# Half of the last prompt tile is gathered with the sample; the second expert table becomes the stationary operand

## The reference, cut to what matters

```
h = h + concat(mixers(rmsnorm(h) @ w_in)) @ w_out
# PEER: 8 heads, 128 x 128 = 16384 experts, 16 chosen per head
q   = (rmsnorm(h) @ wq).reshape(tokens, 8, 2, 64)
s   = einsum('thpd,hpnd->thpn', q, keys)          # 2 x 128 scores per head
top 16 of each side, top 16 of the 16 x 16 sums   # e = i1 * 128 + i2, gate = softmax
act = gelu(sum_d x[t, d] * u_tab[e, d])
h   = h + sum over 8 heads x 16 of gate * act * v_tab[e]
# PLE
h   = h + sigmoid(rmsnorm(h) @ w_gate) * (p @ w_ple)
```

## Time and profile before

| | |
|---|---|
| median of 3 runs | 4154.75 us |
| the profiled execution | 4150.1 us, of it 4148.3 us between the first and the last instruction (the span) |
| TensorE (PE) busy | 98% of the span |
| VectorE (DVE) | 68% |
| GpSimd (POOL) | 44% |
| ScalarE (ACT) | 37% |
| DMA | 858.82 MB, mean 207 GB/s |

### The profile page before, as it was taken

The page is one execution under the profiler, slowest core; times in us unless marked ns, Lnnn a source line. Parts: engine busy times, 40 slices in busy tenths (PEclk is TensorE's granted clock), DMA queues, the critical chain, the costliest instruction groups (busy, mean ns, idle before and its releaser), DMA issues.

```text
span 4148.3 us, 56638 instructions
## 1 busy us (share of the span) xinstructions
PE 4065.6 (98%) x22010; PEld 3474.2 (84%) x22010; DVE 2828.2 (68%) x4773; ACT 1525.8 (37%) x2323; POOL 1844.4 (44%) x1196
## 2 busy tenths in 40 slices
PE   8999999999999999999999999999999999999999
PEld 6788599999999987888477876999999999878883
DVE  5765369936888677777367552799268886677763
ACT  1442155543333333333314312555433333333333
POOL 0131068887777563111001310788877774721110
PEclk9988999999999999999999889999999999999999
DMA  3201156667888999997022011566678889899970
GB/s 122 47 12 47 53 174 216 212 214 243 306 299 306 328 314 335 325 328 266 27 63 38 12 72 41 179 227 212 210 244 308 313 294 339 297 340 326 325 243 23
DMA packets 389291, 858.82 MB, mean 207 GB/s; under 512 B 88352, under 2 KB 236064, under 8 KB 385312
## 3 DMA queue, kind: packets, MB, share of 16 engines
q1 hardware_dynamic: 266144, 578.11, 41.6%
q0 software_dynamic: 67584, 201.57, 14.0%
q10 hardware_dynamic: 55296, 75.52, 5.0%
HBM read 723.51 MB, written 131.54 MB: 206 GB/s over the span
## 4 chain that ended last, share of the span: by engine, by line
PE 75%; DVE 14%; POOL 6%; issue 2%; ACT 2%; DMA 1%; SPq 0%; ACTq 0%; DVEq 0%; POOLq 0%
PE banks L1337 21%; PE banks L1404 20%; PE banks L820 7%; PE banks L1384 4%; PE banks L1260 3%; PE banks L1434 3%; POOL u_stage L2046 3%; PE banks L1278 2%; PE banks L1349 2%; DVE peer_scores L2571 2%; POOL u_stage L2039 1%; DVE peer_scores L2593 1%; PE banks L1113 1%; DVE peer_scores L2568 1%; PE banks L1101 1%
## 5 line engine op out<-in xcount | busy, mean ns | idle before, releaser
L1404 PE MATMUL banks<-v_parts,gated_parts 128*128 128x512 f32 x4608 | 1048.0, 390 | 7.8 <-DVE gated_parts L2730 6.2
L1404 PEld LDWEIGHTS banks<-v_parts,gated_parts 128*128 128x128 f32 x4608 | 865.6, 188 | 189.3 <-issue 9.7
L2031 POOL DMA_INDIRECT peer_gates<-peer_v,u_stage x384 | 533.3, 1389 | 833.2 <-DVE normed L2726 574.8
L1337 PE MATMUL banks<-peer_x_parts,u_parts 128*128 128x448 f32 x3168 | 663.7, 367 | 0.0
L1337 PEld LDWEIGHTS banks<-peer_x_parts,u_parts 128*128 128x128 f32 x3168 | 589.5, 188 | 44.5
L1897 ACT ACTIVATE v_parts<-v_stage 128x1024 fp32r<-128x1024 f32 x256 | 271.4, 1060 | 582.1 <-PE banks L1404 580.3
L2709 DVE TENSOR_TENSOR v_parts<-v_stage,v_parts 128x1024 fp32r<-128x1024 f32 x256 | 313.4, 1224 | 247.2 <-ACT v_parts L1897 247.1
L1337 PE MATMUL banks<-peer_x_parts,low_s 128*128 128x448 f32 x1696 | 398.5, 367 | 0.0
L2039 POOL DMA_INDIRECT u_stage<-gelus,u_stage x256 | 350.5, 1369 | 77.7 <-issue 77.7
L1823 ACT ACTIVATE u_stage<-banks 128x448 f32<-128x448 f32 x256 | 138.9, 542 | 656.5 <-PE banks L1337 641.1
L2686 DVE SCALAR_TENSOR_TENSOR normed<-peer_gates,u_stage,normed 128x1024 f32<-128x1024 f32 x254 | 326.4, 1285 | 60.6 <-DMA peer_gates<-peer_v,u_stage 47.6
(11 more groups left out here) (347 smaller groups left out, 6797.5 us busy)
## 6 DMA issues: line engine op xcount, KB each, us to landing
v_stage<-peer_v SPq DMA_DIRECT2D x256, 512.0 KB, 5.1
u_stage<-peer_ut SPq DMA_DIRECT2D x244, 512.0 KB, 5.4
dense_gelus<-u_stage ACTq DMA_DIRECT2D x256, 224.0 KB
gates<-peer_gates SPq DMA_DIRECT2D x16, 3072.0 KB, 12.1
u_stage<-gates SPq DMA_DIRECT2D x64, 768.0 KB, 6.8
gated<-dense_gelus SPq DMA_DIRECT2D x256, 192.0 KB, 5.7
x<-peer_ut SPq DMA_DIRECT2D x64, 512.0 KB, 5.0
u_raw<-peer_ut SPq DMA_DIRECT2D x64, 512.0 KB, 5.3
```

The costliest lines, as they stand in the source:

```text
L1337: ins = mm(PS[:, d % 2, 0:DW], u_part(n, a, k), XR[:, b, k, DENSE0:TOK], start=(k == 0 and m == 0), stop=(k == KT - 1 and m == 2))
L1404: ins = mm(vo[2 * t + half], HR[:, s, a, t * 128:(t + 1) * 128], VR[:, s, b, half * 512:(half + 1) * 512], start=(j == 0 and m == 0), stop ...
L2031: eng.indirect_dma_start(out=GU[:, t % 4, :], out_offset=None, in_=din["peer_v"].rearrange("l i j d -> (l i j) d"), in_offset=bass.Indirec ...
```

## The change

Three things are changed together.

1. The second half of tile 3 (64 tokens) leaves the dense path and joins the sample (`SPLIT`, `ACROSS`). The gathered tile now has 128 tokens on 128 partitions and `SLOTS` = 128 slots; the sample is scored with all 8 heads, and tile 3 with its heads in two halves, as the sample was before. Tile 3's first 64 tokens stay dense, so 320 columns instead of 384 are gated (`PW3`), scattered (40 units, `GBLK` = 40) and multiplied. The dense rows of the first table keep their 448 columns.
2. In the third stage the roles are exchanged: the table row is stationary in 8 chunks of 128 features, the 320 gated columns move. Per row that is 8 x 3 = 24 matmuls of 320 columns into all 8 PSUM banks. The result stands features by tokens. ACT copies the 8 banks to `VOT`, and TensorE turns them back, tile by tile, in the PLE stage (`down_turned`). Tile 0 is turned there too, because no bank is free before.
3. The gathers are placed anew. `GV` is 4, so 124 slots of tile 0 are added in the second stage. The 128 slots of the gathered tile are added from row 12 on, 8 in 7 rows (`PICKED`). POOL gathers 32 weights first (`WEIGHTS_AHEAD`), then a row and a weight in turn; DVE waits for the weights in 8 groups of 16 instead of once for all. The fold matmuls are gone.

The core of the diff:

```diff
-PW3 = 128 * len(SPREAD)
-GBLK = 48
+PW3 = sum(ACROSS.values())
+GBLK = 40
...
-A_PAIRS = [9, 12, 12, 12, 11]
+A_PAIRS = [13, 13, 13, 11, 7]
 LAST_PAIRS = range(sum(A_PAIRS), PAIRS)
-GV = 17
+GV = 4
...
-SLOTS = 64
+SLOTS = 128
...
+PICKED = 12
+WEIGHTS_AHEAD = 32
...
-        return [m for m in range(SLOTS) if WEIGHED + m * 3 // 2 == j]
+        return [m for m in range(SLOTS) if PICKED + m * 7 // 8 == j]
...
+            def picked_scores():
+
+                for g in range(4):
+                    pe.wait_ge(*bank_free())
+                    b = fill("sc", L, SAMPLE, g)
+                    p, r = g % 2, slice(64 * (g % 2), 64 * (g % 2) + 64)
+                    for n in range(4):
+                        h = 4 * (g // 2) + n
+                        if p == 0:
+                            pe.wait_ge(act_done, at("drained", "qt", L, h, "s"))
+                        for to, c0 in ((slice(0, 64), SEQ), (slice(64, 128), COL[SPLIT] + 64)):
+                            ins = mm(b[to, n * 128:(n + 1) * 128], QT[r, h, c0:c0 + 64], KEYS[r, h, :], start=True, stop=True)
+                    pe.did(ins.then_inc(pe_done, 1), "filled", "sc", L, SAMPLE, g)
...
-            vo = [fill("vo", L, i, half) for i in SPREAD for half in range(2)]
+            vc = [fill("vc", L, k) for k in range(KT)]
             for j in range(NKEYS):
                 s = j % NVB
                 pe.wait_ge(v_low, NKEYS * L + j + 1)
                 pe.wait_ge(h_low, NKEYS * L + j + 1)
-                for t, i in enumerate(SPREAD):
-                    for half in range(2):
-                        for m, (a, b) in enumerate(PARTS):
-                            ins = mm(vo[2 * t + half], HR[:, s, a, t * 128:(t + 1) * 128],
-                                     VR[:, s, b, half * 512:(half + 1) * 512],
-                                     start=(j == 0 and m == 0), stop=(j == NKEYS - 1 and m == 2))
-                        if j == NKEYS - 1:
-                            pe.did(ins.then_inc(pe_done, 1), "filled", "vo", L, i, half)
+                for k in range(KT):
+                    for m, (a, b) in enumerate(PARTS):
+                        ins = mm(vc[k][:, 0:PW3], VR[:, s, b, k * 128:(k + 1) * 128], HR[:, s, a, :],
+                                 start=(j == 0 and m == 0), stop=(j == NKEYS - 1 and m == 2))
+                    if j == NKEYS - 1:
+                        pe.did(ins.then_inc(pe_done, 1), "filled", "vc", L, k)
                 if j < NKEYS - 1:
                     ins.then_inc(v_done, 1)
-                if j == TURN_ROW:
-                    turn(3 * L + 2, GATHER)
-            pe.wait_ge(row_used, ALL_SLOTS * (L + 1))
-            for half in range(2):
-                pe.wait_ge(*bank_free())
-                b = fill("vo", L, SAMPLE, half)
-                ins = mm(b[0:SAM, :], const("fold"), XN[:, 1, half * 512:(half + 1) * 512], start=True, stop=True)
-                pe.did(ins.then_inc(pe_done, 1), "filled", "vo", L, SAMPLE, half)
-
+
+            def down_turned(t):
+
+                i = SPREAD[t]
+                w = ACROSS[i]
+                for half in range(2):
+                    pe.wait_ge(act_done, at("drained", "vc", L, 4 * half + 3))
+                    pe.wait_ge(*bank_free())
+                    b = fill("vo", L, i, half)
+                    for k in range(4):
+                        ins = eng.transpose(b[0:w, k * 128:(k + 1) * 128], VOT[:, 4 * half + k, t * 128:t * 128 + w], ident)
+                    pe.did(ins.then_inc(pe_done, 1), "filled", "vo", L, i, half)
+
+            turn(3 * L + 2, GATHER)
...
+            down_turned(0)
...
-            act.wait_ge(pe_done, at("filled", "vo", L, SAMPLE, 1))
+            act.wait_ge(v_low, NKEYS * (L + 1))
+            for k in range(KT):
+                copy_out(("vc", L, k), VOT[:, k, :], lambda b: b[:, 0:PW3])
+            act.wait_ge(dve_done, at("picked", L))
...
-            for m in range(4, GV):
-                for s in range(SLOTS * (m - 4) // (GV - 4), SLOTS * (m - 3) // (GV - 4)):
-                    gather_weight(s)
-                gather_row(GSLOTS - GV + m)
+            for s in range(WEIGHTS_AHEAD):
+                gather_weight(s)
             for s in range(SLOTS):
                 gather_row(GSLOTS + s)
+                gather_weight(s + WEIGHTS_AHEAD)
...
-                if j == WEIGHED:
-                    dve.wait_ge(weights_gathered, 16 * SLOTS * (L + 1))
-                    dve.did(TT(WGT, WGT, GATE, ALU.mult).then_inc(dve_done, 1))
-                    dve.wait_ge(dve_done, count("dve_done"))
...
+                    if m % CHUNK == 0:
+                        c = slice(m, m + CHUNK)
+                        dve.wait_ge(d_picked[m // CHUNK], 16 * CHUNK * (L + 1))
+                        dve.did(TT(WGT[:, c], WGT[:, c], GATE[:, c], ALU.mult).then_inc(dve_done, 1))
+                        dve.wait_ge(dve_done, count("dve_done"))
...
+            dve.wait_ge(row_used, ALL_SLOTS * (L + 1))
+            dve.did(TT(H[0:SAM, SAMPLE, :], H[0:SAM, SAMPLE, :], XN[0:SAM, 1, :], ALU.add).then_inc(dve_done, 1), "h", 3 * L + 2, SAMPLE)
+            dve.did(TT(H[64:128, SPLIT, :], H[64:128, SPLIT, :], XN[64:128, 1, :], ALU.add).then_inc(dve_done, 1), "picked", L)
             turned(3 * L + 2, GATHER)
-            add_h(L, SPREAD[-1], 1, "vo", 3 * L + 2)
-            for half in range(2):
-                add_h(L, SAMPLE, half, "vo", 3 * L + 2)
+            add_down(1)
+            scale(3 * L + 2, 1)
```

91 lines of the change are left out of this document (54 added, 37 removed).

## The result

The changed kernel takes 4171.45 us (median of 8 runs, 4161.41 to 4187.67), the kernel before 4152.53 us beside it (8 runs, 4143.37 to 4155.88). The ratio is 1.0047, interval 1.0029 to 1.0064: slower by half a per cent, where 4080 us was forecast. The profiled execution took 4161.41 us and has a span of 4159.4 us, against 4148.3 before.

A forecast was written before the change was run, and what follows sets the result against it. TensorE was taken to bound the kernel, and DMA the changed third stage from row 12. Per layer 26.5 + 14.2 - 1 - 1 - 1.2 = 37.5 us, 75 for both, off 4154.75: 4080 us, range 4025 to 4150.

The forecast's parts named there:

- term 2: Third stage: DMA paces from row 12 on, 1.45 MB per row at 385 GB/s, 3.77 us; 168.3 MB in 437 us.
- term 1: Third stage, TensorE: a matmul of 320 columns takes 146 ns, so 24 per table row take 3.50 us against 4.08.
- term 3: Third stage, DVE: 3.31 us of work a row, no bound, with 0.2 to 0.45 us to spare.
- Term 4: Third stage, first gathered row: 32 weights stand before it, so TensorE waits some 18 us (bounds 8 and 22).
- Term 5: Second stage: 8 units go, 14.2 us saved; gathers and DMA fit, 1 us put on irregular waits.
- Term 6: First stage: the half tile is searched last and the new table of pairs costs 1 us, bounds -2 and 8.
- Term 7: Begin of the PLE: turning the sums back and scaling two banks cost 1.2 us more than before.
- The clock: Third stage: TensorE will be slow for some us behind the new wait, but DMA paces the rows and covers it.
- B: Third stage: DMA gives only 345 GB/s, the stage takes 552 us, the whole 4182 us; chance 0.13.
- "DVE busy without a gap": Sign against the forecast: DVE has no gap while DMA is not full, meaning term 3 was too small.

The follow-up runs named there:

- e9_pointer: Changed kernel with the table's low part on DVE by scalar_tensor_tensor, its scalar read from a column of ones in SBUF: 4110.92 us.
- e1: Changed kernel with only the first 32 of a layer's 128 weights gathered and used four times over, 96 commands fewer: 4108.16 us.
- e10: Changed kernel with the second half of the table's low part left out from row 4 on (L2744 on 512 columns): 4104.37 us.
- e2_half_table: Changed kernel with every second row of the second table not loaded in the third stage, from the fifth row on: 4171.41 us.

## Why the prediction was wrong

**The step that failed** is in term 2: "from row 12 on DMA paces the stage", 3.77 us a row. The third stage's sum sets DMA against TensorE (term 1) and DVE (term 3) and has no bound of POOL, though from row 12 on 8 rows and 8 weights have to be gathered in 7 rows. With the price that I had, 1.37 us per gather command from the chain, used in terms 4 and 5 as if it belonged to the command, such a bound would have come out at 2 x 1.37 x 8/7 = 3.13 us and hidden. So the price failed as well: in its place the runs showed 1.57 + 0.30 = 1.87 us per command from row 12 to 96, and POOL's commands as the pace, 4.29 us a row. The earlier trace rows are from a stage in which DVE was busy for 71% of the time; from 1550 to 1800 us of the changed kernel it is 79%. In the third stages of the kernel before 2 of 282 commands took over 2.5 us, in those of the changed kernel 78 of 512.

What it cost: from row 12 to 96 a row takes some 4.29 us instead of 3.77, 84 x 0.52 = 44 us. The third stage is 543.1 us against the 501 forecast, 42 us more, and 540.6 in layer 2. e9_pointer gives 26 us of it back. The other 16 us are the size of term 2: to the end of e9_pointer's stage the 168.3 MB took about 455 us from 1510 on, 370 GB/s on average instead of 385. DMA is not full behind the wait (359 GB/s from 1510 to 1550 us) and in the last rows (229 from 1920 on).

Point by point:

- Term 1, matmul: right (146 ns forecast, 42 us for 288).
- Term 2, DMA: the ceiling was right (381 to 389 GB/s in e1, e9 and e10 at shares of 1.04 and 1.05), the mean over the stage 4% too high, and DMA was not the pace.
- Term 3, DVE: nearly right as a bound on itself (busy for 3.41 us a row, 3.31 forecast), it had gaps (L2762 waited 77.4 us for gathers in layer 1's third stage). What I missed is that its instructions lengthen another engine's.
- Term 4, the wait: 18 forecast, 18.3 and 18.1 measured. Part of this is luck: in layer 1 the 32 weights took 1.47 us each instead of 1.37 (1447.27 to 1494.41 us), and the first of them came 1.8 us earlier in the stage than forecast.
- Term 5, second stage: 7.8 and 7.5 us saved instead of 13.2; the 5.5 us are one wait of 6.0 us at its begin in each layer, gone with LEAD 18. I had the mean rate of the gathers and not the time at which the first rows land.
- Term 6: -2.7 and +0.3 us, the first a little outside the bounds of -2 to 8. Term 7: 1.7 us for 1.2. The sum has a slip here: 0.87 us for the turn of tile 0 were taken off, though they are part of the 527 us against which 501 were set. Without it the term would have been 2.1 us.
- The clock: the stage's 0.94 comes from short stretches at the 1.2 GHz level behind idle times of TensorE, the longest of them around the idle time of 18.3 us (0.56 on average from 1485 to 1504 us). The kernel before, busy throughout, is at 1.00 in the earlier trace rows. The chain from 1550 to 1800 us has no piece of TensorE, so the clock was not what paced the rows there. What it added elsewhere was not separated.

The sum of the misses, against the profiled execution: in layer 1 42.1 (third stage) + 5.4 (second) - 3.7 (first) + 0.5 (PLE) = 44.3 us, in layer 2 39.6 + 5.7 - 0.7 + 0.5 = 45.1 us, and the stages ahead of the experts came out 3.7 us shorter than before: 85.7 us. 4150.1 - 75 = 4075.1 was the forecast for it, 4161.4 its time, 86.3 us apart.

**The rivals.** B, at a chance of 0.13, gave nearly the right time (4182) for the wrong reason, which is luck, and its figure of 353 GB/s is in the trace. Only e2_half_table, fewer bytes and no faster, told it from POOL. "DVE busy without a gap" was the sign I had named for a wrong term 3; DVE does have such stretches in the trace, of several rows, and between them it waits for POOL.

## What to carry to other kernels

Count the commands of every engine that issues gathers against the pace that you forecast, even where it is far from busy before: 56 commands became 134 in the same window. And do not carry a gather command's duration from one stage to another without looking at what DVE does beside it: the command takes 0.95 us when it begins while DVE is idle, and here up to 2.86 us beside it. When DMA shows a share of 1 at fewer GB/s than elsewhere in the same trace, look at who issues.
